# Expert down weights loaded two neighbouring rows to a partition, with the 64-slot products on even and odd columns

## What is computed

```python
def swiglu(t, w_gate, w_up, w_down):
    return (jax.nn.silu(t @ w_gate) * (t @ w_up)) @ w_down

def moe_swiglu(h, w_router, w_gate, w_up, w_down):
    ...
    logits = (t @ w_router).astype(jnp.float32)
    top_vals, top_idx = lax.top_k(logits, TOP_K)
    top_w = jax.nn.softmax(top_vals, axis=-1)
    gates = jnp.sum(jax.nn.one_hot(top_idx, N_EXPERTS, dtype=jnp.float32) * top_w[..., None], axis=1)
    out = jnp.zeros((B * S, Dm), dtype=jnp.float32)
    for e in range(N_EXPERTS):
        ye = swiglu(t, w_gate[e], w_up[e], w_down[e]).astype(jnp.float32)
        out = out + gates[:, e:e + 1] * ye
    return out.astype(h.dtype).reshape(B, S, Dm)
```

## Time and profile before

| | us |
|---|---|
| median of three executions | 1065.04 |
| profiled execution, own time | 1066.72 |
| its span, first to last instruction | 1065.0 |
| TensorE matmul busy | 1029.5 (97%) |
| TensorE weight load busy | 578.6 (54%) |
| VectorE busy | 270.4 (25%) |
| ScalarE busy | 250.7 (24%) |
| GpSimd busy | 54.4 (5%) |
| SyncE's DMA queue, share of the 16 engines' span | 81.9% |
| read from HBM | 341.10 MB, 325 GB/s over the span |

### The profile page before, as it was taken

One profiled execution on the slowest core, in us unless ns is written; L12 is line 12 of the kernel. 1 busy time (PEld: TensorE's weight loads), 2 busy tenths in 40 slices (PEclk: granted clock), 3 DMA queues, 4 the chain that ended last, 5 costly groups with the idle time before them and its releaser, 6 DMA issues.

```text
span 1065.0 us, 22278 instructions
## 1 busy us (share of the span) xinstructions
PE 1029.5 (97%) x9903; PEld 578.6 (54%) x9903; DVE 270.4 (25%) x418; ACT 250.7 (24%) x426; POOL 54.4 (5%) x140
## 2 busy tenths in 40 slices
PE   8999999999999899999999999999999999999675
PEld 8887888888998654444444444444444444332121
DVE  7676544556587310000000000000000000000012
ACT  6765534435676100000000000000000000100111
POOL 4000000000110000000001001000100100100100
PEclk9999999999999899999999999999999999999998
DMA  8477556543638899999999999999999999999994
GB/s 285 172 259 277 187 191 201 160 155 130 230 108 295 306 341 380 419 405 369 401 417 360 379 419 398 369 404 412 347 397 419 377 377 416 417 407 420 420 418 199
DMA packets 125149, 347.24 MB, mean 326 GB/s; under 512 B 7368, under 2 KB 40176, under 8 KB 125056
## 3 DMA queue, kind: packets, MB, share of 16 engines
q1 hardware_dynamic: 119760, 331.64, 81.9%
q0 software_dynamic: 4560, 13.41, 3.7%
q10 hardware_dynamic: 736, 0.80, 0.2%
HBM read 341.10 MB, written 4.72 MB: 325 GB/s over the span
## 4 chain that ended last, share of the span: by engine, by line
PE 86%; DMA 7%; DVE 3%; SPq 2%; issue 1%; ACT 1%; POOL 0%; DVEq 0%; POOLq 0%; ACTq 0%
PE ps L2001 26%; PE ps L2054 13%; PE ps L2005 10%; PE ps L1533 8%; PE ps L1535 8%; PE ps L1534 8%; PE ps L2059 5%; DMA ring<-in_moe_w_down 4%; SPq L822 2%; DMA ring<-in_moe_w_gate 2%; DMA raw_gu<-in_w_in 1%; PE ps L2016 1%; DMA gains<-tok_rows,tok_row 1%; PE ps L2089 1%; PE ps L1540 0%
## 5 line engine op out<-in xcount | busy, mean ns | idle before, releaser
L2001 PE MATMUL ps<-ring,xg 128*32 128x512 f32 (+1 forms) x3072 | 383.8, 553 | 10.3 <-DMA ring<-in_moe_w_up 6.1
L2054 PE MATMUL ps<-ring,moe_ht 128*32 128x512 f32 x1408 | 178.4, 594 | 6.1 <-DMA ring<-in_moe_w_down 6.0
L2005 PE MATMUL ps<-ring,xg 128*32 128x256 f32 x2048 | 176.6, 380 | 0.0
L2001 PEld LDWEIGHTS ps<-ring,xg 128*32 128x32 f32 x3072 | 110.4, 110 | 111.6 <-issue 46.0
L2005 PEld LDWEIGHTS ps<-ring,xg 128*32 128x32 f32 x2048 | 73.2, 110 | 147.2 <-issue 147.2
L1533 PE MATMUL ps<-hi_gu,xt_hi 128*128 128x512 f32 (+1 forms) x352 | 132.6, 377 | 2.2 <-DVE lo_gu L2193 1.3
L1535 PE MATMUL ps<-hi_gu,xt_lo 128*128 128x512 f32 (+1 forms) x352 | 129.2, 367 | 0.0
L1534 PE MATMUL ps<-lo_gu,xt_hi 128*128 128x512 f32 (+1 forms) x352 | 129.0, 367 | 0.0
L1428 ACT ACTIVATE moe_silu<-ps 128x512 f32<-128x512 f32 (+1 forms) x24 | 13.3, 553 | 351.1 <-PE ps L2005 279.7
L2701 DVE TENSOR_TENSOR moe_hidden<-moe_silu,ps 128x512 f32<-128x512 f32 (+1 forms) x24 | 15.2, 632 | 281.6 <-PE ps L2005 170.8
L2691 DVE COPY moe_ht<-ps 128x256 f32<-128x256 f32 (+1 forms) x18 | 7.1, 395 | 295.0 <-PE ps L2027 295.0
(11 more groups left out here) (326 smaller groups left out, 880.4 us busy)
## 6 DMA issues: line engine op xcount, KB each, us to landing
ring<-in_moe_w_down SPq DMA_DIRECT2D x88, 1024.0 KB, 8.3
ring<-in_moe_w_gate SPq DMA_DIRECT2D x56, 1024.0 KB, 8.4
ring<-in_moe_w_up SPq DMA_DIRECT2D x56, 1024.0 KB, 8.9
ring<-in_moe_w_gate SPq DMA_DIRECT2D x40, 768.0 KB, 6.7
ring<-in_moe_w_up SPq DMA_DIRECT2D x40, 768.0 KB, 6.7
raw_gu<-in_dense_w_gate SPq DMA_DIRECT2D x22, 512.0 KB, 3.9
raw_gu<-in_dense_w_up SPq DMA_DIRECT2D x22, 512.0 KB, 4.9
raw_d<-in_dense_w_down SPq DMA_DIRECT2D x11, 1024.0 KB, 4.8
```

The source lines that it names most:

```text
L2001: last = pe.matmul(ps[tile(q), (B_GATE, B_UP)[part], 0:w // 2], xg[:, rows_at, k, tile(g)], weights[:, h * w // 2:(h + 1) * w // 2], start ...
L2005: last = pe.matmul(ps[tile(q), (B_GATE_B, B_UP_B)[part], 0:FC], xg[:, rows_at, k, A_SLOTS:SLOTS], weights[:, q * FC:(q + 1) * FC], start=k ...
L2054: last = pe.matmul(ps[tile(q), B_YA, :], moe_ht[:, at:at + 32], weights[:, h * 512:(h + 1) * 512], start=start, stop=stop)
```

## The change

The destination of a down piece keeps its shape, but partition p now receives the rows 2p and 2p + 1 of the piece's 256, which lie next to each other in HBM, as one run of 8 KB. The half k of a slot holds the rows 2i + k. So block b of `down` multiplies every second row, and the hidden values must come in that order:

- A slots: the matmul of line 2001 streams every second column of the piece (`h:w:2`, a step of 8 bytes) in place of one half of it. The hidden values then lie contiguous in PSUM and SBUF, and the transposes of line 2016 are as before. `a_at` takes j and h in the other order, to match.
- B slots: the products of line 2005 stay contiguous, and the transpose of line 2027 takes every second column of its 256.
- The first 512 columns of p = 0: `pick_hidden` (line 1891) takes every second column of each 256.

```diff
@@ -154,7 +154,7 @@
 
         if c < 0:
             return b * SLOTS
-        h, j = divmod(b, width(p, c) // (2 * P))
+        j, h = divmod(b, 2)
         return j * P + h * A_SLOTS
@@ -820,7 +820,7 @@
                 if part == DOWN:
                     r0 = col0(p, c) + i * FC
                     sp.dma_start(ring[:, slot, :].rearrange("p (k n) -> p k n", k=2),
-                                 expert_rows(moe_w_down, e)[r0:r0 + FC, :].rearrange("(k p) n -> p k n", p=P)
+                                 expert_rows(moe_w_down, e)[r0:r0 + FC, :].rearrange("(p k) n -> p k n", p=P)
                                  ).then_inc(ring_loaded[slot], 16)
@@ -1886,7 +1886,7 @@
                 for k in range(4):
-                    at = slice(k * P, (k + 1) * P)
+                    at = slice(k // 2 * FC + k % 2, (k // 2 + 1) * FC, 2)
@@ -1999,7 +1999,7 @@
                         last = pe.matmul(ps[tile(q), (B_GATE, B_UP)[part], 0:w // 2], xg[:, rows_at, k, tile(g)],
-                                         weights[:, h * w // 2:(h + 1) * w // 2], start=k == 0, stop=k == KT - 1)
+                                         weights[:, h:w:2], start=k == 0, stop=k == KT - 1)
@@ -2024,7 +2024,7 @@
                     for j in range(2):
-                        last = pe.transpose(ps[:, B_HTB, j * P:j * P + some.stop], moe_hidden[some, 512 + j * P:512 + (j + 1) * P],
+                        last = pe.transpose(ps[:, B_HTB, j * P:j * P + some.stop], moe_hidden[some, 512 + j:3 * FC:2],
                                             ident[some, some])
```

## The result

The changed kernel takes 1078.15 us (median of four executions, 1075.43 to 1079.29) beside 1064.47 us before; the ratio is 1.0118, with a 95% interval of 1.0104 to 1.0131. It is slower, by about 1.2%. The ratios of this document are those on record and are not the quotients of the medians (here 1.0129). They leave out the slow executions, those of 1086.65 and 1086.67 us of the kernel before and one of 5775.04 us of the run with strided loads. The forecast of 1064.2 us was wrong, and the measured time lies outside its range.

What follows compares the result with a forecast made beforehand. TensorE was taken to bound the kernel until about 956 us, transfers from about 885 to 1043 us. The 8 KB runs save 0.8 us and strided streams and loads cost nothing: median 1064.2 us, range 1062.4 to 1072.

Steps and rivals of the forecast that it cites:

- part 2: Line 2001 streaming every second column: taken to cost nothing, bounded above by +258 us and a little more in the tail.
- the rival on the other side: Strided stream slows line 2001 from 376 to 956 us, about 1072 us at 3%; chance 0.16, shared with slower strided loads.
- my nearest row: Dense stage's float32r matmuls read 512 adjacent numbers in 0.23 us; taken as showing line 2001's strided stream costs nothing.
- the prediction's count of steps: TensorE's steps up to 956 us: 192 of 512 columns at 0.86 us, 144 of 384 at 0.645 us, 258 us in all.
- The end of the stretch in which TensorE's time counts: TensorE's time was said to count in full until about 956 us, where place 6's gate and up products end.
- the transfers' stretch from 885 us: A byte's transfer time was said to count in full from about 885 to 1043 us.
- Part 1: Down pieces in 8 KB packets for 4 KB: gain 0.8 us, bounds 0.3 and 1.1 us, nothing before 885 us.
- The rival of slow large packets: 8 KB down packets at 56 ns per KB, 3.5 us per down piece: +32 us, 1097 us; chance 0.04.
- Part 3: Strided array loads at lines 2027 and 1891, 36 of 140 ns and 16 of 192 ns: taken to cost nothing.
- the bound of 8.1 us: Upper limit for the loads of lines 2027 and 1891 if each doubled and none of it were hidden.
- the doubled stream: Line 2001's stream taking twice as long: 258 us plus 38 in place 7, some 15 idle, about 1345 us.

Runs made afterwards that it cites:

- the run with strided loads: Kernel before with contiguous streams, transposes taking even and odd columns in chunks of 1024, and 8 KB runs except in chunks of 768; ratio 0.9999.
- the runs above: Changed kernel with line 2001 streaming every fourth number, 1368.19 us, or every third, 1214.32 us, in place of every second.
- the stride alone: Changed kernel with down pieces back in 4 KB runs, strided streams and transposes kept, so rows of w_down meet wrong hidden values; ratio 1.0112.
- places 0 to 5 alone: Kernel before with the change at places 0 to 5 only, the first 512 columns of place 0 left in the old order; ratio 1.0108.
- The runs by place: Kernel before with the change at places 6 and 7 only, ratio 0.9982 and again 0.9990, or at places 0 to 5 only, ratio 1.0108.
- runs alone: Kernel before with only the down pieces' 8 KB runs added, so rows of w_down meet wrong hidden values; ratio 0.9994, again 0.9997.
- every fourth number: Changed kernel with line 2001 streaming at a step of 16 bytes in place of 8, so products use other weights; 1368.19 us.

## Why the prediction was wrong

**The step that failed is part 2, the price of the strided stream: forecast 0, measured about +0.045 us for a step of 512 columns (0.04 to 0.05) and +0.035 for 384.** The risk was named as the rival on the other side, with its place (line 2001, while TensorE sets the pace), its point (the first per cent) and 2.6 us for each 1%. Its chance of 0.16 and the value taken were wrong. The mistake is in how I read my nearest row. I took the dense stage's `float32r` stream, 512 numbers in 0.23 us, and wrote that twice as many pieces "is just the rate that one stream of the dense stage keeps up". That takes the dense stage's 0.23 us twice over in 0.43 us, and two times 0.23 is 0.46: even the rounded figures did not agree. Read to another digit, over fifteen matmuls in a row in the trace of the kernel before:

```profile
120.26 0.39 PE L1533 MATMUL ps<-hi_d,ht_hi 128*128 128x512 f32 x1
...
123.66 0.39 PE L1533 MATMUL ps<-hi_gu,xt_hi 128*128 128x512 f32 x1
```

3.40 us / 15 is 0.2267 us for 128 groups of 16 bytes, 1.77 ns each, the same price as in the runs above. A strided step touches 256 groups twice: 4 x 0.2267 = 0.907 us. By the prediction's own argument the trace of before gave 5% and not 0. That both streams are held up by the same thing no run shows.

With 48 steps per place that is 32 x 0.045 + 16 x 0.035 = 2.0 us, and with the slower loads about the 2.1 us that a place has grown. By the prediction's count of steps the whole is 192 x 0.045 + 144 x 0.035 = 13.7 us, of which place 6's 2.0 do not count (below): 11.7 us. From the first products of the experts to those of place 6 the changed kernel takes 11.4 us more than the one before, the stride alone and places 0 to 5 alone 12.4 each, and the ratio 1.0108 is 11.5 us. The medians of the result differ by 13.7 us; that this equals the full count is chance, as the four executions alone lie 3.9 us apart.

**The end of the stretch in which TensorE's time counts.** I put it at 956 us and let it overlap with the transfers' stretch from 885 us. A stretch cannot charge both. Once the queue of issued pieces is never empty, slower products only shorten the backlog. The runs by place bear this out. (The two chain rows that the prediction calls the gate products of places 2 and 3 are the up products of their second chunks; the distance of 90.8 us holds all the same.) In the changed kernel's own trace, 10.6 us of delay had built up at the first long group of place 6 (911.30 us beside 900.71 in this row of the chain before):

```profile
900.71 6.87 PE ps L2001 x64
```

It was 12.9 us after place 6's last up products and 9.1 at the last down products. So what place 6 lost never reached the end. The other 1.5 us are of the size of the runs' gain and of the scatter between executions: the trace of the stride alone, on 4 KB runs, is 11.4 us later than before at place 6 and 11.5 at the last down products, but that of places 0 to 5 alone, also on 4 KB runs by then, is 16.2 us later and then 15.3.

**Part 1, the runs.** The mechanism was right: one packet for 8 KB, a packet time of about 311 ns for the forecast 313, a higher rate in the last stretch (419 GB/s for 416 from 895 to 1040 us; from 985 to 1010 us, where not only down pieces land, runs alone have 422 for 419 and the changed kernel 420), and nothing before it. In the time of the kernel the gain is not clear of noise: forecast 0.8 us, measured 0.06% and 0.03% (0.6 and 0.3 us) with intervals that include none. The rival of slow large packets is out; its sum was also a little low, since 8 x 56 ns is 0.45 us for a packet and 3.6 us for a down piece, not 3.5.

**Part 3, the strided loads.** Forecast nothing, measured 60 ns more for each of line 2027 (200 ns for 140), 2.2 us if all of it showed. With the A transposes strided as well a place pays 0.2 us. Line 1891's 16 loads take 196 ns for 192. A small miss, well inside the bound of 8.1 us.

**The sum and the doubled stream.** The price of 1345 us for a stream twice as slow was sound: at every fourth number, 2.1 times as slow, the kernel took 1368 us.

## What to carry to other kernels

A float32 stream with a step of 8 bytes is not free on TensorE: at steps of up to 16 bytes, count the 16-byte groups it touches at 1.76 ns each against its numbers at 0.84 ns, and the longer wins. Put such a step where few bytes are read, or where the engine waits anyway: the same edit costs 11.5 us (1.0108 of 1065) at places 0 to 5 and nothing that shows at places 6 and 7. Compare traces by stretches and not by their ends: here they start 0.9 us and more apart before the change has acted. And when a forecast rests on two rates being equal, work the nearest row out over many instructions before calling them so; 5% lay in the second digit.

## What the runs showed of the hardware

I had not expected that the dense stage's contiguous `float32r` matmuls (0.2267 us for 512 columns at a granted clock of 1.00) run at the very price per 16 bytes that the strided float32 streams show. That they are limited by the same thing is an inference from the equal number; no run changed them. The Trainium skill (SBUF — State Buffer, "Door 1: The DMA port swizzle") says that two hits in each line of 16 bytes give full speed. The runs fit lines of 16 bytes, though larger ones would fit as well, and they agree on one hit being the steep case (1.80 us for 0.86), but two hits fall 5% short here. By the rule taken literally the changed kernel would have taken 1064 us; it took 1078.
